# Encoder layer on one Trainium2 core: four-quarter products replaced by seven half-depth block products in three branches, and a pooling branch moved and split over two engines

## The reference, cut to what matters

```python
z = h @ w_in
ya = gelu_u * spatial(gelu_v)                  # 512 wide
yb = (pooled_g @ b_wg[g]) * b_scale            # 4 groups of 128, windows 2, 4, 8, 16
yc = attention(...)                            # 512 wide
yd = bg * short_conv(cg * xd)                  # 512 wide
gates = sigmoid(z[..., OFF_G:])                # 4 branches x 1024
merged = gates[0]*(ya @ p_a) + gates[1]*(yb @ p_b) + gates[2]*(yc @ p_c) + gates[3]*(yd @ p_d)
y = merged @ w_o                               # then LayerNorm, router, 16 experts, LayerNorm
# pooling of one group with window w: (sum of w neighbours) / count - itself
```

## Time and profile before

| | us |
|---|---|
| median of three runs (2687.79 to 2690.64) | 2688.86 |
| the profiled execution | 2690.6 |
| its span | 2688.8 |
| TensorE busy | 2546.9 (95%) |
| VectorE busy | 910.3 (34%) |
| ScalarE busy | 433.0 (16%) |
| GpSimd busy | 407.9 (15%) |

### The profile page before, as it was taken

How to read it: one execution, slowest core, us unless ns; L and a number is a source line. 1 busy time by engine, 2 the same in 40 slices (tenths; PEclk the granted TensorE clock), 3 DMA queues, 4 the chain that set the end, 5 groups by cost and what they waited for, 6 DMA issues and landing times.

```text
span 2688.8 us, 33063 instructions
## 1 busy us (share of the span) xinstructions
PE 2546.9 (95%) x13492; PEld 1825.5 (68%) x13492; DVE 910.3 (34%) x1687; ACT 433.0 (16%) x811; POOL 407.9 (15%) x510
## 2 busy tenths in 40 slices
PE   6999999999999999999999999659999999999993
PEld 3555666677777777777777744348788878887882
DVE  2566775322333323533232257740000000000004
ACT  1224775100100000001010011100000000000003
POOL 1334443000044000000000012101111111111102
PEclk8999999999999999999999999769999999999997
DMA  7002005201011101111021042537877787778754
GB/s 261 24 16 79 2 2 167 78 24 40 16 51 28 39 24 32 33 39 47 24 72 38 24 173 102 186 127 247 277 255 256 246 276 255 256 246 276 255 197 166
DMA packets 217053, 333.15 MB, mean 124 GB/s; under 512 B 7024, under 2 KB 97424, under 8 KB 216960
## 3 DMA queue, kind: packets, MB, share of 16 engines
q1 hardware_dynamic: 208912, 309.88, 33.8%
q0 software_dynamic: 8048, 21.97, 3.2%
HBM read 305.58 MB, written 26.25 MB: 123 GB/s over the span
## 4 chain that ended last, share of the span: by engine, by line
PE 87%; POOL 3%; DVE 3%; DMA 3%; ACT 2%; issue 1%; SPq 0%; POOLq 0%; ACTq 0%; DVEq 0%
PE PS L1715 39%; PE PS L1901 21%; PE PS L1921 8%; PE PS L1627 6%; PE PS L1805 5%; POOL RT L621 3%; PE PS L1914 2%; DMA R<-in_w_ada_dram 2%; PE PS L1669 1%; ACT RT L823 1%; PE PS L1878 1%; DVE top_i L1453 0%; PE PS L1560 0%; DVE RT L1456 0%; DVE RT L1451 0%
## 5 line engine op out<-in xcount | busy, mean ns | idle before, releaser
L1901 PE MATMUL PS<-RQ,R 128*128 128x160 f32 x3072 | 427.7, 299 | 0.0
L1901 PEld LDWEIGHTS PS<-RQ,R 128*128 128x128 f32 x3072 | 420.7, 190 | 0.0
L1715 PE MATMUL PS<-RQ,RT 128*128 128x320 f32 x1040 | 287.0, 432 | 0.0
L1715 PE MATMUL PS<-R,RW 128*128 128x320 f32 x1040 | 286.7, 432 | 0.0
L1715 PEld LDWEIGHTS PS<-RQ,RT 128*128 128x128 f32 x1040 | 197.2, 190 | 81.7 <-issue 0.2
L1715 PEld LDWEIGHTS PS<-R,RW 128*128 128x128 f32 x1040 | 197.2, 190 | 81.5
L1921 PE MATMUL PS<-R,RQ 128*128 128x512 f32 x512 | 224.0, 595 | 0.0
L1486 DVE TENSOR_TENSOR RQ<-RQ,PS 128x160 f32<-128x160 f32 x128 | 41.1, 321 | 516.4 <-ACT RQ L979 516.4
L1715 PE MATMUL PS<-RY,RT 128*128 128x320 f32 x768 | 212.6, 432 | 0.0
L1715 PEld LDWEIGHTS PS<-RY,RT 128*128 128x128 f32 x768 | 145.9, 190 | 60.8
L1627 PE MATMUL PS<-R,RW 128*128 128x512 f32 (+1 forms) x480 | 177.1, 526 | 3.5 <-ACT RW L807 3.5
(11 more groups left out here) (254 smaller groups left out, 2556.8 us busy)
## 6 DMA issues: line engine op xcount, KB each, us to landing
R<-in_e_w_dram SPq DMA_DIRECT2D x80, 2048.0 KB, 10.5
RV<-in_e_w_dram SPq DMA_DIRECT2D x16, 2048.0 KB, 7.9
RW<-in_w_in_dram SPq DMA_DIRECT2D x39, 512.0 KB, 4.0
R<-in_w_ada_dram SPq DMA_DIRECT2D x16, 1024.0 KB, 8.0
RT<-in_w_in_dram SPq DMA_DIRECT2D x13, 512.0 KB, 5.3
RT<-in_p_all_dram SPq DMA_DIRECT2D x24, 256.0 KB, 3.2
RY<-in_x_dram SPq DMA_DIRECT2D x10, 512.0 KB, 3.3
R<-in_x_dram SPq DMA_DIRECT2D x10, 512.0 KB, 3.3
```

The source lines that it names most:

```text
L1715: last = pe.matmul(dst[:, h, :], a[:, k, :], b[:, k, HN * h:HN * h + HN], start=k == 0, stop=k == KH - 1)
L1901: last = pe.matmul(ab_ps[j % 2][:, m, :], w_half[c][:, k, (j % 4) * P:(j % 4 + 1) * P], xgT[:, k, :], start=k == 0, stop=k == KD - 1)
```

## The change

- In the gate pairs of branches 0 and 3, and in three of the four of branch 1, the four products with `p` become seven products of half depth (256), `Q1, Q2, Q6, Q7, Q4, Q5, Q3`, in the same scheme as the `w_in` products. They come after the seven `P` blocks (order BOTH).
- For that VectorE makes four sums of quarters of the two `p` tiles in each such pair (`p_sums`, after `P5`), four sums of quarters of `y` once for a branch (`y_block_sums`), and puts the seven products together (`p_summed`); ScalarE copies `Q1` out twice. The gates multiply the sums in SBUF (`d1, d2, d3`) and no longer PSUM. The second gate quarter has a place of its own (`c4`).
- The `b` pairs go behind the gates of branch 3. GpSimd pools groups 0 and 2, VectorE pools group 1 (inside the second `b` pair, after `P6`) and group 3 (inside the first gate pair of branch 1, after `P6`).
- The first gate pair of branch 1 has the order MIXED: seven `P` blocks, the eight mix products, then the four plain products with `p`. Its first plain product waits until ScalarE has copied the last mix product.
- The six rows of constants are loaded after the last product of the last pair.

The diff, cut to its core:

```diff
-        pairs += [beside("u", COL_U, i) for i in range(2)] + [beside("b", COL_B, i) for i in range(2)] + gate_pairs(0)
+        pairs += [beside("u", COL_U, i) for i in range(2)] + gate_pairs(0)
...
-        pairs += gate_pairs(3) + gate_pairs(1)
+        pairs += gate_pairs(3) + [beside("b", COL_B, i) for i in range(2)] + gate_pairs(1)
...
+        MIX = tuple(f"mix{q}" for q in range(8))
+        MIXED = PLAIN + MIX + P_USE
+        BOTH = PLAIN + ("Q1", "Q2", "Q6", "Q7", "Q4", "Q5", "Q3")
...
+            pr.mixed = pr.branch == 1 and pr.i == 0
+            pr.both = pr.gate and pr.branch != 2 and not pr.mixed
+            pr.order = BOTH if pr.both else MIXED if pr.mixed else GATED if pr.gate else PLAIN
...
# SyncE, after w_o and x have been issued behind the last pair's P3
+            sp.wait_ge(block_done, made(late, late.last_p))
+            sp.wait_ge(mod2_rows_stored, 16)
+            for dst, values in ((g1_b[0], mod_rows[0, 0:D]), (ln1g_b, ln1_g), (ln1b_b, ln1_b), (sc2_b[0], mod_rows[0, 2 * D:3 * D]),
+                                (sh2_b[0], mod_rows[0, D:2 * D]), (g1_b[1], mod_rows[1, 0:D])):
+                everywhere(dst, values).then_inc(row_constants_in, 16)
...
# GpSimd
-            for g, w in enumerate(WINDOWS):
+            for g, w in ((0, WINDOWS[0]), (2, WINDOWS[2])):
...
# ScalarE, behind the four sigmoids of a pair
+                if pr.both:
+                    m, src, _ = pr.block["Q1"]
+                    act.wait_ge(block_done, m + 1)
+                    act.wait_ge(block_used, m)
+                    act.activation(d1, src, ACT.Copy)
+                    act.activation(d2, src, ACT.Copy).then_inc(block_used, 1)
+                if pr.mixed:
+                    for q, name in enumerate(MIX):
...
+                        act.activation(quarter_of(y1, q // 2, q % 2), src, ACT.Copy, scale=colT[:, 76 + q // 2:77 + q // 2]).then_inc(block_used, 1)
...
# VectorE
             def gated(pr, k):
...
+                if pr.both:
+                    d, need = ((d1, "Q2"), (d1, "Q4"), (d3, "Q5"), (d2, "Q3"))[k]
+                    dve.wait_ge(block_used, made(pr, need))
+                    own.did(dve.tensor_tensor(c, c, d, ALU.mult))
+                    own.settle()
...
             def gate_pair(pr, nxt):
                 for name in pr.order[1:]:
                     if name in P_USE:
                         gated(pr, P_USE.index(name))
-                    else:
+                    elif name in PLAIN:
                         summed(pr, name)
+                    elif name in BOTH and name != "Q1":
+                        p_summed(pr, name)
+                    if name == "P6" and pr.mixed:
+                        pooling(3)
+                    if name == "P7" and pr.both and pr.i == 0:
...
+                        y_block_sums(pr.branch)
+                    if name == "P5" and pr.both:
+                        p_sums(pr)
                     if nxt and name == "P5":
                         weight_sums(nxt, 0)
                     if nxt and name == "P3":
                         weight_sums(nxt, 1)
+                    for k in {"Q6": (0,), "Q5": (1, 2), "Q3": (3,)}.get(name, ()):
+                        gated(pr, k)
+                if pr.mixed:
+                    y_block_sums(pr.branch)
+
+            def pooling(g):
...
+                for at, lo, m in SEGS:
+                    own.did(dve.tensor_copy(z[:, at:at + m], y1[:, g, lo:lo + m]))
...
+                own.did(dve.tensor_tensor(sum_a[:, 1:n], z[:, 0:n - 1], z[:, 1:n], ALU.add))
+                src, dst, a = sum_a, sum_b, 1
+                while 2 * a < w:
...
+                    own.did(dve.tensor_tensor(dst[:, 2 * a:n - 2 * a], src[:, a:n - 3 * a], src[:, 3 * a:n - a], ALU.add))
...
+                for at, lo, m in SEGS:
+                    own.did(dve.scalar_tensor_tensor(out=y1[:, g, lo + 8:lo + m - 8], in0=src[:, at + 8:at + m - 8], scalar=1.0 / w,
+                                                     in1=z[:, at + 8:at + m - 8], op0=ALU.mult, op1=ALU.subtract))
...
# TensorE
+                depth = a.shape[1]
                 for h in range(2):
-                    for k in range(KH):
-                        last = pe.matmul(dst[:, h, :], a[:, k, :], b[:, k, HN * h:HN * h + HN], start=k == 0, stop=k == KH - 1)
+                    for k in range(depth):
+                        last = pe.matmul(dst[:, h, :], a[:, k, :], b[:, k, HN * h:HN * h + HN], start=k == 0, stop=k == depth - 1)
...
+                        elif name == "p11":
+                            pe.wait_ge(block_used, pr.block["mix7"][0] + 1) if pr.mixed else None
```

More of the change, by code:

```diff
@@ L341, in build @@
         y_of = {0: y0, 1: y1, 2: y0, 3: y0}
+        y_sums = {b: [r[:, 1280 * i:1280 * i + 1280].rearrange("p (k n) -> p k n", k=KB // 2) for i in range(3)]
+                  for b, r in ((0, RV), (3, RV), (1, RY))}
+        Y_SUMS_SEEN = {0: 0, 3: 4, 1: 8}
         last_in_bank = [-1] * 4
@@ L354, in build @@
         GATED = ("P1", "P2", "P6", "p11", "P7", "P4", "P5", "p21", "P3", "p22", "p12")
-        LATE = PLAIN + ("p11", "p21", "p22", "p12")
         P_USE = ("p11", "p21", "p22", "p12")
+        MIX = tuple(f"mix{q}" for q in range(8))
+        MIXED = PLAIN + MIX + P_USE
+        BOTH = PLAIN + ("Q1", "Q2", "Q6", "Q7", "Q4", "Q5", "Q3")
         g0 = p0 = m0 = 0
         for n, pr in enumerate(pairs):
-            if pr.branch == 1 and pr.i == 0:
-                mix_blocks = [next_block(4) for q in range(8)]
             pr.n, pr.g0, pr.m0 = n, g0, m0
-            pr.order = LATE if pr is late else GATED if pr.gate else PLAIN
+            pr.mixed = pr.branch == 1 and pr.i == 0
+            pr.both = pr.gate and pr.branch != 2 and not pr.mixed
+            pr.order = BOTH if pr.both else MIXED if pr.mixed else GATED if pr.gate else PLAIN
+            pr.q0 = 4 * sum(q.both for q in pairs[:n])
+            pr.last_p = "Q3" if pr.both else "p12"
+            pr.c4 = c4 if pr.both else c4_beside_pooling if pr.mixed else c1
             pr.block = {name: next_block(3 if pr.kind == "u" else 4) for name in pr.order}
@@ L474, in load_p @@
                 if pr.n:
-                    sp.wait_ge(block_done, max(made(q, "p12") for q in pairs[:pr.n] if q.gate))
+                    sp.wait_ge(block_done, max(made(q, q.last_p) for q in pairs[:pr.n] if q.gate))
                 for f in range(2):
@@ L554, in load_half @@
                   .then_inc(expert_half_in[c], 16)
-            sp.wait_ge(block_done, made(late, "p12"))
+            sp.wait_ge(block_done, made(late, late.last_p))
             load_half(0, 0)
@@ L1226, in summed @@
                     dst = z_conv[:, 1:1 + HT].rearrange("p (a n) -> p a n", a=2)
-                elif name == "P4" and pr.gate and pr is not late:
-                    if pr.branch != 2:
-                        dve.wait_ge(merge_added, pr.m0 + 1)
-                    else:
-                        dve.wait_ge(block_used, made(pr, "p11"))
+                elif name == "P4" and pr.branch == 2:
+                    dve.wait_ge(block_used, made(pr, "p11"))
                 add = dve.tensor_tensor(dst, c, src, ALU.add)
@@ L1294, in plain_pair @@
                     summed(pr, name)
+                    if name == "P6" and pr is B_PAIRS[1]:
+                        pooling(1)
                     if name == "P5":
```

134 lines of the change are left out of this document (88 added, 46 removed).

## The result

The changed kernel takes **2673.02 us** (median, 2672.26 to 2675.93) against 2687.97 us (2687.74 to 2690.64) of the kernel before in the same comparison: a ratio of 0.9941, interval 0.9930 to 0.9952, 15 us faster. In a second comparison it was 2670.76 against 2689.82 us: 0.9938 (0.9924 to 0.9952), 19 us faster. The forecast was 2672.0 us, within 2668.5 to 2678.5.

A forecast was written before the change was run, and what follows sets the result against it. The prediction took TensorE's matmuls, 0.269 us an instruction, to bound the stretch that the change touches. Its terms, -23.7 + 3.3 + 3.5 = -16.9 us, gave a median of 2672.0 us, range 2668.5 to 2678.5.

The forecast's parts named there:

- (a) The products: In 11 gate pairs, seven half-depth blocks replace four full ones: 2.15 us less TensorE time each, a gain of 23.7 us.
- the rival on the slower side: Each of 77 half-depth blocks has a fixed cost f; 0.4 us gives 2703 us; chance 0.05 together with another rival.
- (b) VectorE's added work: In the changed pairs, VectorE's extra sums end 5.3 us after the last product, hidden inside the stretch: nothing.
- (c) the sums of `y`: Once in a branch, four VectorE subtractions of about 1.5 us each, 6.0 us in all: cost nothing.
- (d) The moved pairs: The `b` pairs moved behind branch 3's gates: TensorE's work the same, waits behind seven blocks, cost nothing.
- (e) The pooling in the mixed pair: VectorE's pooling of 10.5 us plus 4.5 us lost to GpSimd delays the first plain product: 3.3 us lost.
- the lower bound of 1.1 us: Loss in the mixed pair if VectorE loses no time to GpSimd: only ScalarE's last copy shows, 1.1 us.
- The wait of about 1 us at a mix product: Sign of a right forecast: TensorE waits about 1 us at a mix product, 2 us ahead of the first plain product.
- (f) The end: Ahead of `w_o`, VectorE ends 5.3 us after the last product instead of 1.8: 3.5 us lost; clock effect taken at 0.
- (g) The constants: Six transfers issued after the last product take some 16 us, needed 22 us after it: hidden by 6 us.
- no lost turns in (e): Rival: in the mixed pair VectorE wins or GpSimd is done earlier, loss 1.1 us; sum -19.1, 2669.8 us; chance 0.2.
- the rival of the stalling Q phase: Rival: VectorE's lag in the half-depth products uses up the banks; 11 waits of about 1 us, about 2684; chance 0.05.

The follow-up runs named there:

- experiment 5: Changed kernel plus four more VectorE additions of 128x640 behind the sum of `Q3` in ten new pairs: 2672.62 us, ratio 0.9939 to the kernel before.
- Experiment 4: Changed kernel with four plain products in each pair again, new pair order, shared pooling and mixed pair kept: 2691.75 us, ratio 1.001 to the kernel before.
- experiment 2: Changed kernel with the four additions of VectorE's pooling of group 3 made twice: 2676.96 us, ratio 0.9957 to the kernel before.
- experiment 9: On top of experiment 8, the even mix products come first and the first plain product waits for their last copy alone: 2663.62 us, ratio 0.9911.
- experiment 1: Changed kernel without VectorE's pooling of group 3 in the mixed pair: 2672.18 us, ratio 0.9938 to the kernel before.
- experiments 6: Changed kernel with the four plain products back in the last pair alone: 2669.53 us, ratio 0.9931 to the kernel before.
- experiment 8: Changed kernel with gates reordered in the last pair and `w_o` begun ahead of the last sums: 2664.80 us, ratio 0.9909 to the kernel before.
- experiment 7: Changed kernel with the second gate behind `Q4` instead of `Q5` in every new pair: 2671.16 us, ratio 0.9932 to the kernel before.

## Why the prediction was right, point by point

- **(a) The products**: right. A half-depth block takes 2.16 us to the start of the next (1440.73 to 1442.89 in experiment 5), 8 instructions each; the page counts 88 fewer. Experiment 4 takes the products back, and the gain goes with them. So falls the rival on the slower side: its fixed cost f is nothing that shows (2.16 us against 8 x 0.269 = 2.15), where it needed 0.22 us.
- **(b) VectorE's added work** and **(c) the sums of `y`**: right, both at nothing. VectorE ended 5.3 us behind the last product of a pair as worked out; the sums of `y` took 1.49 us each (1.5). Experiment 5 shows that 3.4 us more a pair cost nothing either.
- **(d) The moved pairs**: right; experiment 4 has no place for more than 0.3 us outside the mixed pair.
- **(e) The pooling in the mixed pair: the term that was mis-sized**, 3.3 us forecast and 1.3 measured. The chain was as told, and stage by stage it reads: start t = 13.9 (13.8); end of the pooling 26.2 (28.8); sum of `P3` done 32.2 (34.7); copies done 39.9 (41.9); first plain product 39.9 (42.0). The 2.6 us lie in the pooling alone; the eight copies took 6.98 us instead of 6.4 and so took 0.6 of it back. Undisturbed the pooling is 0.90 + 1.52 + 4.62 + 0.40 + 1.52 + 0.40 = 9.4 us and not 10.5 (the additions from VectorE's pooling of group 1 and experiment 2, the copies from that of group 1, the row at 1327.97): the eight edge operations take 0.8 us, where the sum has 1.4, and a second copy has no fixed part that shows. The lock then cost VectorE 12.3 − 9.4 = 2.9 us and not 4.5. That the two take turns was forecast and came true. But I let each us that GpSimd had left cost VectorE one, and it cost less: 2.36 us in the three additions (6.98 against 4.62) for subtractions that take 2.96 by themselves, and 0.56 in the copies and the first addition for the rest of the scaling and the four edge operations, 0.66 + 0.69 by themselves. With the smaller price the chain from VectorE to the last copy ends within 0.1 us of where that copy would end anyway, which was the lower bound of 1.1 us (1.28 in experiment 9 less 0.12 in experiment 1). The wait of about 1 us at a mix product, named as a sign of a right forecast, was not there.
- **(f) The end**: right, 3.4 us of 3.5, shown by experiments 6 and 8. The clock's part was taken at 0 against the kernel before. The first tile took 15.51 us there and 15.4 to 16.2 in the six traces with the gap of 6.38 us, so it is −0.1 to 0.7 us. Both kernels pay more than that: behind a gap of 0.92 us that tile takes 13.83 us.
- **(g) The constants**: right, hidden. VectorE's first step behind `w_o` waited for TensorE (the row at 1558.17, 22.3 us after the last product); the transfers were issued from 1535.88 to 1538.99 and each landed 4 to 9 us after its issue, the last at 1547.0.

The sum should have been −23.7 + 1.3 + 3.4 = −19.0, which is the rival *no lost turns in (e)* (−19.1, 2669.8 us) by its time, though not by its reason: turns were lost, and cost 0.1 us. The profiled execution, forecast at 2673.7 us, took 2672.26. That the first median, 2673.02, stands 1.0 us from the forecast and 3.2 from 2669.8 is luck, of the spread of the runs: the second one, 2670.76, stands between them, and the stretch misses the forecast by some 2 us (19.05 against 16.9).

Some of the prediction's own sums slip: the parts that GpSimd has left, 0.5 + 0.7 + 3.0, are 4.2 us and not 4.5; 42.0 − 38.8 is 3.2 and not 3.3; and the rival of the stalling Q phase, 16.9 less 11, leaves 5.9 us, which is 2683 and not 2684. None of them changes a conclusion.

The Trainium skill, page "SBUF — State Buffer", section "SBUF: two separate sides", which the prediction named beside the price of the lock, says of a VectorE operation with two operands in SBUF and a GpSimd operation that whichever starts first has the shared port pair for its whole instruction, and that the other blocks. The rows agree: GpSimd's last edge operation, 0.17 us when free (0.69 for four), took 1.48 beside VectorE's first addition, and VectorE's third, 1.54 when free (4.62 for three), took 3.51 beside GpSimd's subtraction. What I drew from it, that VectorE loses all the time that GpSimd's work takes, stands in no row: it lost 2.9 of some 4.3 us.

## What to carry to other kernels

Trading products for additions pays the full time of the products as long as TensorE sets the pace and the other engine's lag at the end of a round stays within the free banks (some 8.5 us here still did, more was not tried); its price shows only where a stage ends, so look there for what the next stage really needs (here the first tile needed two additions fewer, and the early start was worth 7 us, 1.8 of it by the clock, over a third of what the change had given). When a moved piece of work has to fit beside other work, work out both its length and the point from which it counts: a chain that ends at the same place as a cheaper one, as here, costs next to nothing (0.1 us), and what is added to it from there on costs one for one (6.2 us for 6.2 in experiment 2). Price small operations from rows of several of them back to back, not from the nearest larger one.

## What the runs showed that was not expected

- **Both engines lose by the lock, and not equally.** In the overlap VectorE lost 2.9 us (12.3 against 9.4) and GpSimd 4.3 (2.44 + 5.51 against 0.69 + 2.96). VectorE's two copies were held too: 1.41 us against 0.90.
- **The price of the clock behind a gap does not follow from the gap's length alone.** The first tile of `w_o` took 13.83 us at 1.00 throughout behind 0.92 us of idle time (experiment 8). Behind 3.02 us it took 15.50 or 15.51 in three traces (the kernel before, experiments 4 and 6); the clock was at 1.00 when `w_o` began and fell to 0.50 some 1 to 1.5 us later. Behind 6.38 us it took 15.4 to 16.2 in six traces; the clock was at 0.50 when `w_o` began and came back 3 to 5 us later. The 16.25 behind 5.35 (experiment 7) is hardly outside of these, so these runs show no clear order among gaps of 3 to 6 us. What sets the moment at which the clock comes back is not shown by these runs.
